# The TensorE program of a two-direction chunked scan, written as two counted loops, with the changes on VectorE and ScalarE that go with it

## The chip, the cores and the metric

The kernel runs on one core of one Trainium2 chip. The metric is the device time of one execution in microseconds (us). Three runs of the kernel before took 2723.7, 2718.01 and 2723.88 us; the median is 2723.7. The profiled execution took 2724.22 us by itself, and its trace spans 2722.2 us.

## The reference

The program is two transformer layers followed by one block of another kind, all in float32 on 256 tokens of width 1024. The change touches one piece of that last block, a recurrent scan over 16 heads of 64 channels, in two directions, first over 256 context tokens and then over 256 output tokens:

```python
def wkv_scan(s0, scan_in):
    def step(s, inp):
        w, kk, a, k, v, r = inp
        sa = jnp.einsum('dbhij,dbhj->dbhi', s, kk)
        s = s * w[..., None, :] - sa[..., :, None] * (kk * a)[..., None, :] + v[..., :, None] * k[..., None, :]
        return s, jnp.einsum('dbhij,dbhj->dbhi', s, r)
    return lax.scan(step, s0, scan_in)
...
    s_ctx, y_c = wkv_scan(s0, scan_c)
    _, y_x = wkv_scan(s_ctx, scan_x)
```

Only the outputs over the 256 output tokens (`y_x`) are used; of the context the scan hands on the state alone.

## The kernel before

The scan does 64 tokens at a time, so it has 8 steps `h`: 0 to 3 over the context (both directions `d` at once), 4 to 7 over the output tokens. The 16 heads lie as 8 chunks `c` of two heads, one head in partitions 0 to 63 and the other in 64 to 127, so a product for one direction is 16 small matmuls (`tile`, 64x64 by 64x64). Each float32 matmul appears in the trace as two weight loads (PEld) and two matmuls (PE), which makes four instructions on TensorE.

One step has these parts. `scores` multiplies keys, removal keys and a unit matrix; VectorE writes the part below the diagonal into `LA` (`left_matrices`, line 2644). GpSimd starts the inverse of a triangular matrix from it (`begin_inverse`, line 2985), VectorE transposes that start (line 2677), and then five levels follow, each a ring over four engines: TensorE multiplies `LA` by the present inverse (`left_products`), VectorE masks the product (line 2682, shown as L2400, the helper `tt`), TensorE multiplies again (`level_products`), ScalarE copies the result out of PSUM (line 2281), VectorE transposes it (line 2687). Four of the five levels are already a counted loop on TensorE (line 1923), whose waits compare a semaphore with a register; all its other waits before compare with a constant. When the inverse is done (`inverse_done`), `corrected_values` uses it, ScalarE copies the values out (line 2240), `state_update` sums the new state in PSUM, and VectorE adds it to the old state and scales it by the decay of the chunk (`new_state`, line 2665: two additions of 512 columns, one product of 1024). `uncorrected` of the next step needs that state. In steps 4 to 7 there are also `reads` (the masked matrices `RD`, line 2706) and the outputs (`first_outputs`, `last_outputs`). Two tiny copies on VectorE fetch the decay of the next step (`chunk_decay`, line 2572) between the fourth and the fifth level.

Every engine works its program in order. PSUM has 8 banks in two rings of four (`act_ring`, emptied by ScalarE, and `dve_ring`, emptied by VectorE); TensorE opens banks in turn and waits until a bank is free. On TensorE the eight steps stand one behind the other in the code; on the other engines too, before and after. The order of a step on TensorE:

```python
        for h in STEPS:
            read = h - 1 in X_STEPS
            if read:
                y = first_outputs(h - 1)
            if h:
                corrected_values(h - 1, h)
            if read:
                last_outputs(h - 1, y)
            if h:
                state_update(h - 1)
            ...
            scores(h, 0)
            scores(h, 1)
            ...
            inverse(h, left)
```

## Time and profile before

| | us |
|---|---|
| median of 3 runs (lowest, highest) | 2723.7 (2718.01, 2723.88) |
| the profiled execution, its own time | 2724.22 |
| its span in the trace | 2722.2 |
| TensorE busy | 2476.4 |
| VectorE busy | 1305.2 |
| ScalarE busy | 558.6 |
| GpSimd busy | 540.3 |

The page gives the busy time of each engine, the queues, the chain of work that ended last, and the costliest groups of instructions. The scan starts its first scores about 1517 us into the span and its last outputs are added at 1877 us. "Q8" below is the queue that the page calls q8 instruction: packets of the program itself that are fetched while it runs, 120 of them in this execution with 1.97 MB, so 16.4 KB each. A wait in a timeline is put in brackets with the idle time before it and what released it; "issue" stands for idle time for which the profile shows no releaser.

### The profile page before, as it was taken

The numbers are of one execution on the slowest core, as the hardware profiler recorded it, in microseconds if no ns is written. First come the engines' busy times: TensorE is split into PE (matmuls) and PEld (weight loads), VectorE is DVE, ScalarE is ACT, GpSimd is POOL, SyncE is SP. The second block draws the span as 40 slices with busy tenths as digits, with TensorE's granted clock in tenths as the row PEclk, the third lists the DMA queues.
The fourth block names the chain that finished last, engine by engine and source line by source line (L and its number), as shares of the span: only waits on it lengthen the run. The fifth ranks groups of instructions, "written<-read, shape, count | busy, mean of one in ns | idle before, by whom it ended". The sixth has DMA issues, their size and how long they took to land.

```text
span 2722.2 us, 43824 instructions
## 1 busy us (share of the span) xinstructions
PE 2476.4 (91%) x18216; PEld 1682.6 (62%) x18216; DVE 1305.2 (48%) x2899; ACT 558.6 (21%) x1285; POOL 540.3 (20%) x434
## 2 busy tenths in 40 slices
PE   8999999999999999998999787889998987787787
PEld 6688786476886853444677777878866533333333
DVE  2873310037732101147447554545228677777665
ACT  1243000013330000114333233222002111111111
POOL 0000000000000000000012665530003455544552
PEclk9999999999999999999999999999999999988999
DMA  5333333344233335423353011003348999999997
GB/s 189 148 120 124 131 151 152 133 168 157 102 124 143 149 148 218 162 93 135 144 201 78 18 32 34 18 3 133 124 170 319 414 415 421 421 421 422 422 421 319
DMA packets 91227, 523.70 MB, mean 192 GB/s; under 512 B 39728, under 2 KB 39728, under 8 KB 43440
## 3 DMA queue, kind: packets, MB, share of 16 engines
q0 software_dynamic: 39360, 277.51, 25.0%
q1 hardware_dynamic: 51696, 243.80, 24.0%
q8 instruction: 120, 1.97, 0.3%
q14 instruction: 51, 0.42, 0.0%
HBM read 511.85 MB, written 9.44 MB: 191 GB/s over the span
## 4 chain that ended last, share of the span: by engine, by line
PE 66%; DVE 13%; DMA 10%; issue 4%; ACT 2%; DVEq 2%; POOL 1%; POOLq 1%; ACTq 0%; SPq 0%
PE psum L523 35%; PE psum L1598 23%; DMA mem<-weights,mem 10%; DVE mem L2887 4%; PE psum L2045 3%; DVE mem L2400 2%; PE psum L765 2%; PE psum L539 1%; PE psum L2017 1%; POOL mem L2937 1%; DVE mem L2687 1%; ACT mem L2281 1%; POOL mem L3037 1%; DVEq L2521 0%; PE psum L1608 0%
## 5 line engine op out<-in xcount | busy, mean ns | idle before, releaser
L523 PE MATMUL psum<-mem 128*128 128x256 f32 (+10 forms) x4248 | 954.5, 397 | 7.5 <-DVE mem L1079 3.3
L1598 PE MATMUL psum<-mem 64*64 64x64 f32 (+6 forms) x12192 | 882.1, 273 | 85.6 <-DVEq L2683 23.2
L1598 PEld LDWEIGHTS psum<-mem 64*64 64x64 f32 (+3 forms) x12192 | 687.7, 154 | 279.1 <-issue 172.0
L523 PEld LDWEIGHTS psum<-mem 128*128 128x128 f32 (+5 forms) x4248 | 691.9, 182 | 262.5 <-issue 168.0
L2045 PE MATMUL psum<-mem 128*128 128x512 f32 x1024 | 496.4, 642 | 123.2 <-ACT mem L2364 123.1
L2045 PEld LDWEIGHTS psum<-mem 128*128 128x128 f32 x1024 | 205.0, 205 | 408.4 <-issue 241.0
L3037 POOL DMA_INDIRECT mem<-weights,mem x256 | 315.2, 1231 | 528.2 <-PE psum L2045 267.3
L2887 DVE CUSTOM_DVE_ANT_0 mem<-mem 128x1024 f32<-128x1024 f32 x256 | 307.3, 1224 | 138.8 <-DMA mem<-weights,mem 131.9
L2937 POOL TENSOR_TENSOR mem<-mem 128x512 f32<-128x512 f32 (+3 forms) x148 | 205.6, 1402 | 169.2 <-DVEq L2652 134.2
L2400 DVE TENSOR_TENSOR mem<-psum,mem 128x512 f32<-128x512 f32 (+1 forms) x145 | 97.3, 680 | 219.1 <-PE psum L1598 188.3
L2400 DVE TENSOR_TENSOR mem<-mem 128x512 f32<-128x512 f32 (+7 forms) x211 | 135.6, 651 | 89.0 <-ACTq L2153 67.5
L2359 ACT ACTIVATE mem<-mem 128x4 f32<-128x4 f32 (+2 forms) x70 | 14.4, 205 | 510.2 <-DVE mem L2891 510.2
L1284 DVE TENSOR_TENSOR mem<-mem 128x512 f32<-128x512 f32 x32 | 22.1, 692 | 193.7 <-ACTq L982 193.7
L1071 DVE SCALAR_TENSOR_TENSOR mem<-mem 128x256 f32<-128x256 f32 x240 | 105.6, 481 | 9.4 <-issue 0.9
L1304 POOL DMA_DIRECT2D mem<-vectors x1 | 0.5, 537 | 539.9 <-DVEq L1291 539.9
L1287 DVE TENSOR_TENSOR mem<-psum,mem 128x512 f32<-128x512 f32 x8 | 5.5, 692 | 205.5 <-PE psum L523 205.5
L1306 POOL MEMSET mem<- 128x256 f32 x1 | 0.3, 311 | 493.9 <-ACT mem L985 493.9
L3000 POOL DMA_DIRECT2D rates_dram<-mem x16 | 14.2, 892 | 405.9 <-DVEq L2570 405.9
L2364 ACT ACTIVATE mem<-mem 128x128 f32<-128x128 f32 x256 | 82.4, 390 | 32.7 <-DVE mem L2400 31.3
L2281 ACT ACTIVATE mem<-psum 128x512 f32<-128x512 f32 x80 | 47.8, 597 | 149.0 <-PE psum L1598 149.0
L2687 DVE STREAM_TRANSPOSE mem<-mem 128x512 f32<-128x512 f32 x64 | 45.5, 711 | 50.2 <-ACTq L2282 50.2
L837 ACT ACTIVATE mem<-psum 128x512 f32<-128x512 f32 (+4 forms) x88 | 45.7, 569 | 104.4 <-PE psum L523 100.2
(244 smaller groups left out, 1307.8 us busy)
## 6 DMA issues: line engine op xcount, KB each, us to landing
mem<-weights SPq DMA_DIRECT2D x100, 2048.0 KB, 7.4
rates_dram<-mem POOLq DMA_DIRECT2D x16, 512.0 KB, 5.0
mem<-rates_dram SPq DMA_DIRECT2D x32, 256.0 KB, 4.5
mem<-weights SPq DMA_DIRECT2D x7, 1024.0 KB, 6.7
mem<-weights SPq DMA_DIRECT2D x2, 2176.0 KB
mem<-weights,mem POOLq DMA_INDIRECT x256, 27.1
mem<-weights SPq DMA_DIRECT2D x2, 1536.0 KB, 8.5
mem<-weights SPq DMA_DIRECT2D x2, 1152.0 KB
```

Source lines behind the costliest of these rows:

```text
L523: ins = pe.matmul(out, lhsT, rhs, start=start, stop=stop, skip_group_check=skip)
L765: ins = pe.matmul(b, mg[:, k, t * P:(t + 1) * P], w[half][:, k, :], start=k == 0, stop=k == 7)
L1071: v.scalar_tensor_tensor(cacc[:, c, :], src, w, cacc[:, c, :], ALU.mult, ALU.add)
L1598: ins = pe.matmul(out, lhsT, rhs, start=start, stop=stop, skip_group_check=skip)
L2045: last = pe.matmul(psum[:, 4 + 2 * t + half, :], diag[:, n % DIAGS, :], rows_uv[buf_of[n]][:, D + half * 512:D + (half + 1) * 512], start= ...
L2281: A((Dm if j < LEVELS - 1 else DTm)[:, d * 512:(d + 1) * 512], banks[d], ACT.Copy)
L2364: A(diag[:, n % DIAGS, :], ident, ACT.Copy, scale=g1[:, n:n + 1]).then_inc(diag_ready.sem, 1)
L2400: return v.tensor_tensor(o, a, b, op)
L2687: v.transpose(DTm[:, d * 512:(d + 1) * 512], Dm[:, d * 512:(d + 1) * 512])
L2887: v.tensor_tensor_reduce(u, u, h2[:, t, :], 1.0, 0.0, ALU.mult, ALU.add, actp[:, n:n + 1])
L2937: return pool.tensor_tensor(o, a, b, op)
L3037: pool.indirect_dma_start(out=rows_uv[buf_of[n]], out_offset=None, in_=UV, in_offset=bass.IndirectOffsetOnAxis(ap=eidx_u[:, n:n + 1], axis ...
```

## The change

TensorE's program for the scan becomes two counted loops, one of four context steps and one of four output steps, with the loop over the levels inside. A step now begins with `scores` and ends with `state_update`, so the last step also updates the state and turns values that nobody uses; ScalarE and VectorE take those banks before they report the scan as done. Every wait in the loops compares with a register computed from the loop counters, and stands in an instruction of its own that also counts up a semaphore (`until`). So that each turn of a loop is alike: two more banks of `dve_ring` are opened and released in the output steps, the values of the next step are copied to a fixed place by ScalarE (`VS`, two copies of 512 columns, after the second level), and the old state enters the sum in PSUM through two 512-column products with the unit matrix (`kept_state`). VectorE then scales the sum straight out of PSUM (two operations of 512 columns in place of three). The decay of the next chunk is fetched by ScalarE behind its exponentials, no longer by VectorE in the inverse. VectorE's order within a level changes: transpose and mask of direction 0, then transpose and mask of direction 1. In the output steps the first transposes come before the masking of the second direction's reads.

```diff
...
+    VS = [zwa, sb2(512, base + 4096)]
...
+        step = {}
+
+        def at(signal, n, i=0):
+            return signal.sem, step["i"] * (step["steps"] * signal.per) + signal.at(step["h"] - n, i)[1]
+
+        def until(*waits):
+            for sem_, value in waits:
+                pe.wait_ge(sem_, value)
+            pe.sem_inc(pe_step, 1)
+
+        def bank(ring, tag):
+            tags = ring.filled["post"]
+            tags.append(tag)
+            n = len(tags) - 1
+            until((ring.free, step["i"] * step[ring] + ring.count("post", n)))
+            return ring.banks[:, n % 4, :]
+
         terms_done = [0]
 
         def mark(last):
             last.then_inc(term_full.sem, 1)
             terms_done[0] += 1
-            return terms_done[0]
+            return term_full.sem, step["i"] * step["terms"] + terms_done[0]
+
+        def staged_values(side, d, c):
+            return VS[d].rearrange("p (c n) -> p c n", c=8)[64 * side:64 * side + 64, c, :]
...
+        def kept_state():
+            b = [bank(dve_ring, "St") for _ in range(2)]
+            for d in range(2):
+                last = mm(b[d], ident, St[:, 512 * d:512 * d + 512], True, False, skip=True)
+            return b, mark(last)
+
+        def state_update(b, kept):
+            until(kept, at(u_ready, 0, 0))
             for c in range(8):
                 for head in range(2):
-                    tile(b[0], 0, c, head, 0, 0, own(TOK), half_of(nU), c == 0, False)
-                    last = tile(b[1], 1, c, head, 1, 0, other(TOK), half_of(VT_TOK), c == 0, False)
-            pe.wait_ge(term_full.sem, mark(last))
-            pe.wait_ge(*u_ready.at(h, 1))
+                    tile(b[0], 0, c, head, 0, 0, own(TOK), half_of(nU), False, False)
+                    last = tile(b[1], 1, c, head, 1, 0, other(TOK), half_of(VT_TOK), False, False)
+            until(mark(last), at(u_ready, 0, 1))
...
                 for d in range(2):
-                    pe.wait_ge(inverse_ready.sem, j * 2 + (2 * LEVELS * h + d + 1))
-                    pe.sem_inc(pe_step, 1)
+                    until(level(inverse_ready, 2, d))
                     left_products(left, d)
                 for d in range(2):
-                    pe.wait_ge(left_ready.sem, j * 2 + (2 * LEVELS * h + d + 1))
-                    pe.wait_ge(inverseT_ready[d].sem, j + (LEVELS * h + 1))
-                    pe.sem_inc(pe_step, 1)
+                    until(level(left_ready, 2, d), level(inverseT_ready[d], 1))
                     level_products(products[d], d, DTm, ARm)
...
-        for h in STEPS:
-            read = h - 1 in X_STEPS
+        def scan_step(read):
+            until(at(pq_ready, 0), at(k_ready, 0))
+            scores(0)
+            scores(1)
             if read:
-                y = first_outputs(h - 1)
-            if h:
-                corrected_values(h - 1, h)
+                reads(0)
+            uncorrected()
             if read:
-                last_outputs(h - 1, y)
-            if h:
-                state_update(h - 1)
-            if h == 0:
-                pe.wait_ge(*shift_parts_used.at(0, len(RW_ORDER) - 1))
-                values_product(h)
-            pe.wait_ge(*pq_ready.at(h))
-            pe.wait_ge(*k_ready.at(h))
-            scores(h, 0)
-            scores(h, 1)
-            if h in X_STEPS:
-                reads(h, 0)
-                uncorrected(h)
-                reads(h, 1)
-            else:
-                uncorrected(h)
-            left = [dve_ring.open(pe, "held") for _ in range(2)]
-            pe.wait_ge(*qt_ready.at(h, 1))
-            inverse(h, left)
-        y = first_outputs(7)
-        corrected_values(7)
-        last_outputs(7, y)
+                reads(1)
+            left = [bank(dve_ring, "held") for _ in range(2)]
+            until(at(qt_ready, 0, 1))
+            inverse(left)
+            if read:
+                for _ in range(2):
+                    bank(dve_ring, "held")
+                y = first_outputs()
+            kept = kept_state()
+            corrected_values()
+            if read:
+                last_outputs(y)
+            state_update(*kept)
+
+        pe.wait_ge(*shift_parts_used.at(0, len(RW_ORDER) - 1))
+        values_product(0)
+        for first, count, read, act_banks, dve_banks, terms in ((0, 4, False, 12, 8, 3), (4, 4, True, 12, 16, 5)):
+            filled = [len(ring.filled["post"]) for ring in (act_ring, dve_ring)]
+            with pe.Fori(0, count) as i:
+                step.update({"i": i, "h": first, "steps": 1, act_ring: act_banks, dve_ring: dve_banks, "terms": terms})
+                done = terms_done[0]
+                scan_step(read)
...
+            if h:
+                act.drain()
+                A(chunk_decays[h % 2][:, 0:8], R0[h % 2][:, 0, :, 63], ACT.Copy)
+                A(chunk_decays[h % 2][:, 8:16], R0[h % 2][:, 1, :, 0], ACT.Copy)
...
+                if j == 1 and h < 7:
+                    for d in range(2):
+                        A(VS[d].rearrange("p (c n) -> p c n", c=8), zv[:, :, starts(h + 1)[d]:starts(h + 1)[d] + 64], ACT.Copy)
...
+        for d in range(2):
+            take("Vt")
+            act.sem_inc(act_step, 1)
+        act.drain().then_inc(act_ring.free, 2)
...
-        def new_state():
+        def new_state(h):
             for d in range(2):
-                st = St[:, d * 512:(d + 1) * 512]
-                done(tt(st, take("St"), st, ALU.add))
-            v.drain()
-            tt(ch(St), ch(St), bc(Wc, 2, 64), ALU.mult)
+                kept = bc(chunk_decays[(h - 1) % 2][:, 8 * d:8 * d + 8], 2, 64)
+                done(tt(dir_(St, d), take("St").rearrange("p (c n) -> p c n", c=8), kept, ALU.mult))
             v.drain().then_inc(state_ready.sem, 1)
 
-        def inverse(h, between):
-            left = dve_ring.held(2)
+        def first_inverse(h):
             for d in range(2):
                 v.wait_ge(*inverseT_ready[d].at(h))
                 v.transpose(Dm[:, d * 512:(d + 1) * 512], DTm[:, d * 512:(d + 1) * 512])
                 v.drain().then_inc(inverse_ready.sem, 1)
+
+        def inverse(h):
+            left = dve_ring.held(2)
             for j in range(LEVELS):
                 for d in range(2):
+                    if j:
+                        v.wait_ge(*inverse_ready.at(h, 2 * j + d))
+                        v.transpose(DTm[:, d * 512:(d + 1) * 512], Dm[:, d * 512:(d + 1) * 512])
+                        v.drain().then_inc(inverseT_ready[d].sem, 1)
                     v.wait_ge(*left_full.at(h, 2 * j + d))
                     tt(dir_(ARm, d), left[d].rearrange("p (c n) -> p c n", c=8), bc(level[:, j + 1, 1 - d, :], 1, 8), ALU.mult)
                     v.drain().then_inc(left_ready.sem, 1)
-                if j < LEVELS - 1:
-                    for d in range(2):
-                        v.wait_ge(*inverse_ready.at(h, 2 * j + 2 + d))
-                        v.transpose(DTm[:, d * 512:(d + 1) * 512], Dm[:, d * 512:(d + 1) * 512])
-                        v.drain().then_inc(inverseT_ready[d].sem, 1)
-                between(j)
-            v.sem_inc(dve_ring.full, 2)
-            v.drain().then_inc(dve_ring.free, 2)
+            held = 2
+            if h in X_STEPS:
+                dve_ring.held(2)
+                held += 2
+            v.sem_inc(dve_ring.full, held)
+            v.drain().then_inc(dve_ring.free, held)
+
+        def read_matrices(h, d):
+            for head in range(2):
+                masked(f"reads{head}", RD[head], d, incl[:, d, :])
 
         for h in STEPS:
             if h - 1 in X_STEPS:
@@ -2696,22 +2737,21 @@
             if h in X_STEPS:
                 receptance(h)
             if h:
-                new_state()
-            v.tensor_copy(Wc, Wnext)
+                new_state(h)
             for d in range(2):
                 left_matrices(h, d)
             if h in X_STEPS:
-                for d in range(2):
-                    for head in range(2):
-                        masked(f"reads{head}", RD[head], d, incl[:, d, :])
+                read_matrices(h, 0)
+            first_inverse(h)
+            if h in X_STEPS:
+                read_matrices(h, 1)
                 v.drain().then_inc(intra_r_ready.sem, 1)
-
-            def next_rates(j):
-                if h < 7 and j == 3:
-                    chunk_decay(h + 1)
-
-            inverse(h, next_rates)
+            inverse(h)
         add_outputs(7)
+        for d in range(2):
+            take("St")
+            v.sem_inc(dve_step, 1)
+        v.drain().then_inc(dve_ring.free, 2)
```

The order on VectorE in an output step before, from the last state operation to the second level (L2400 that waits for dve_bank_full is `new_state` or the masking of `reads`, L2642 is `left_matrices`, L2677 the first transposes, L2687 the transposes of a level, L2400 that waits for left_full the mask of a level):

```order
L2400 TENSOR_TENSOR mem<-mem 128x1024
L2700 COPY mem<-mem 128x16
L2642 COPY_PREDICATED mem<-mem,psum 128x512 [waits dve_bank_full]
L2642 COPY_PREDICATED mem<-mem,psum 128x512 [waits act_bank_full]
L2642 COPY_PREDICATED mem<-mem,psum 128x512 [waits dve_bank_full]
L2642 COPY_PREDICATED mem<-mem,psum 128x512 [waits act_bank_full]
L2400 TENSOR_TENSOR mem<-psum,mem 128x512 [waits dve_bank_full] x4
L2677 STREAM_TRANSPOSE mem<-mem 128x512 [waits inverseT_ready0]
L2677 STREAM_TRANSPOSE mem<-mem 128x512 [waits inverseT_ready1]
L2400 TENSOR_TENSOR mem<-psum,mem 128x512 [waits left_full] x2
L2687 STREAM_TRANSPOSE mem<-mem 128x512 [waits inverse_ready] x2
L2400 TENSOR_TENSOR mem<-psum,mem 128x512 [waits left_full] x2
```

The same place after (L2435 is the helper that was L2400, L2709 the first transposes, L2718 those of a level):

```order
L2677 COPY_PREDICATED mem<-mem,psum 128x512 [waits act_bank_full]
L2435 TENSOR_TENSOR mem<-psum,mem 128x512 [waits dve_bank_full] x2
L2709 STREAM_TRANSPOSE mem<-mem 128x512 [waits inverseT_ready0]
L2709 STREAM_TRANSPOSE mem<-mem 128x512 [waits inverseT_ready1]
L2435 TENSOR_TENSOR mem<-psum,mem 128x512 [waits dve_bank_full] x2
L2435 TENSOR_TENSOR mem<-psum,mem 128x512 [waits left_full] x2
L2718 STREAM_TRANSPOSE mem<-mem 128x512 [waits inverse_ready]
L2435 TENSOR_TENSOR mem<-psum,mem 128x512 [waits left_full]
L2718 STREAM_TRANSPOSE mem<-mem 128x512 [waits inverse_ready]
L2435 TENSOR_TENSOR mem<-psum,mem 128x512 [waits left_full]
```

The masking of two of the four reads moved behind the first transposes, and in a level the masks and transposes now alternate.

On TensorE before, from the end of one context step's inverse to the next step's scores (first row: `corrected_values`; u_ready: `state_update`; 128x2x64: `scores`):

```order
L1598 MATMUL psum<-mem 64x64 [waits act_bank_free,inverse_done,u0_ready]
L1598 MATMUL psum<-mem 64x64 x29
L1598 MATMUL psum<-mem 64x64 [waits u0_ready,inverse_done]
L1598 MATMUL psum<-mem 64x64 x33
L1598 MATMUL psum<-mem 64x64 [waits u_ready,dve_bank_free]
L1598 MATMUL psum<-mem 64x64 x31
L1598 MATMUL psum<-mem 64x64 [waits u_ready,term_full]
L1598 MATMUL psum<-mem 64x64 x31
L1598 MATMUL psum<-mem 128x2x64 [waits dve_bank_free,act_bank_free,k_ready,pq_ready]
L1598 MATMUL psum<-mem 128x2x64 x15
```

The end of the same part after, where the loop (L1984) goes back; the scores stand at the head of the loop's body:

```order
L1599 MATMUL psum<-mem 64x64 [waits inverse_done,u0_ready]
L1599 MATMUL psum<-mem 64x64 x33
L1805 REGISTER_ALU
L1599 MATMUL psum<-mem 64x64 [waits term_full,u_ready]
L1599 MATMUL psum<-mem 64x64 x31
L1805 REGISTER_ALU
L1599 MATMUL psum<-mem 64x64 [waits term_full,u_ready]
L1599 MATMUL psum<-mem 64x64 x31
L1984 REGISTER_ALU
L1984 COMPARE_AND_BRANCH
```

And the head of that body after, up to the first scores, which the branch leads back to:

```order
L1984 ISA
L1805 ISA [waits pq_ready,k_ready]
L1805 REGISTER_ALU [waits dve_bank_free]
L1805 ISA [waits dve_bank_free]
L1805 REGISTER_ALU [waits act_bank_free]
L1599 MATMUL psum<-mem 128x2x64 [waits act_bank_free]
L1599 MATMUL psum<-mem 128x2x64 x15
```

Ahead of the scores there are now a branch and a row of register operations and waits. Counted out, the body of the context loop is 354 matmuls and 75 other instructions, 1491 in all with four to a matmul; that of the output loop 482 matmuls and 101 others, 2029 in all. The body of the inner loop is 64 matmuls, some 265 instructions.

## Rows read from the trace of the kernel before

**Rows 1.** The page: TensorE in all, and the queue that fetches the program.

```profile
PE 2476.4 (91%) x18216; PEld 1682.6 (62%) x18216; DVE 1305.2 (48%) x2899; ACT 558.6 (21%) x1285; POOL 540.3 (20%) x434
...
q8 instruction: 120, 1.97, 0.3%
```

**Rows 2.** Busy time by stretch: us, engines busy (instructions), granted clock, DMA share, GB/s.

```profile
1510.00:1880.00 370.00, 299.24 (x9616) 285.57 (x9617) 186.55 (x274) 111.63 (x177) 183.15 (x131) 0.95 0.11 27
...
1743.00:1751.00 8.00, 5.65 (x128) 5.47 (x127) 4.09 (x6) 2.93 (x4) 6.80 (x7) 0.79 0.35 70
1751.00:1769.00 18.00, 15.60 (x500) 15.13 (x497) 11.47 (x18) 4.21 (x8) 13.32 (x8) 1.00 0.01 1
```

**Rows 3.** Timeline of one level (start, us, engine, instructions, idle before).

```profile
1575.40 4.03 PE L1598 MATMUL psum<-mem 64*64 64x64 f32 x128 [0.53 <-DVEq L2683]
...
1577.24 0.71 DVE L2687 STREAM_TRANSPOSE mem<-mem 128x512 f32<-128x512 f32 x1 [1.30 <-ACTq L2282]
1577.52 0.60 ACT L2281 ACTIVATE mem<-psum 128x512 f32<-128x512 f32 x1 [0.34 <-PE psum L1598]
1578.17 0.71 DVE L2687 STREAM_TRANSPOSE mem<-mem 128x512 f32<-128x512 f32 x1 [0.22 <-ACTq L2282]
1579.00 1.50 DVE L2400 TENSOR_TENSOR mem<-psum,mem 128x512 f32<-128x512 f32 x2
...
1580.00 4.03 PE L1598 MATMUL psum<-mem 64*64 64x64 f32 x128 [0.57 <-DVEq L2683]
```

**Rows 4.** The chain that ended last, over the fifth level and a context step's end.

```profile
1589.01 0.69 DVE mem L2400
...
1589.79 2.11 PE psum L1598 x64
...
1593.05 1.17 PE psum L1598 x60
...
1594.92 8.47 issue
1603.39 1.30 POOLq L2994
```

**Rows 5.** Timeline of the same boundary: TensorE's gap, the state and the scores.

```profile
1598.07 4.46 PE L1598 MATMUL psum<-mem 64*64 64x64 f32 x95 [1.08 <-issue]
1598.81 1.29 DVE L2400 TENSOR_TENSOR mem<-psum,mem 128x512 f32<-128x512 f32 x2 [8.29 <-PE psum L1598]
...
1600.19 1.23 DVE L2400 TENSOR_TENSOR mem<-mem 128x1024 f32<-128x1024 f32 x1
1601.54 0.17 DVE L2700 COPY mem<-mem 128x16 f32<-128x16 f32 x1
1601.65 0.73 DVE L2642 COPY_PREDICATED mem<-mem,psum 128x512 f32<-128x512 uint32 x1
```

**Rows 6.** The groups of VectorE's two small copies, 1510 to 1880 us.

```profile
L2574 DVE COPY mem<-mem 128x8 f32<-128x8 f32 x7 | 5.2, 748 | 1.2 <-issue 0.5
...
L2575 DVE COPY mem<-mem 128x8 f32<-128x8 f32 x7 | 1.1, 161 | 0.0
```

**Rows 7.** Timeline of an output step, from GpSimd's start of the inverse to the first mask.

```profile
1740.30 2.59 POOL L2937 TENSOR_TENSOR mem<-mem 64x512 f32<-64x512 f32 x2 [0.24 <-issue]
...
1743.59 1.29 DVE L2400 TENSOR_TENSOR mem<-psum,mem 128x512 f32<-128x512 f32 x2 [2.96 <-PE psum L1598]
...
1745.91 7.56 PE L1598 MATMUL psum<-mem 64*64 64x64 f32 x192 [2.35 <-DVEq L2678]
1747.91 0.69 DVE L2400 TENSOR_TENSOR mem<-psum,mem 128x512 f32<-128x512 f32 x1 [1.35 <-PE psum L1598]
```

**Rows 8.** The chain over an output step's end, from the outputs to the scores.

```profile
1774.70 1.75 issue
1776.45 3.02 PE psum L1598 x124
1779.46 1.01 issue
...
1782.44 0.67 DVE mem L2400
...
1785.26 0.74 DVE mem L2642
```

**Rows 9.** The instruction queue from 1591 to 1606 us.

```profile
q8 instruction: 4, 0.07, 2.0%
```

**Rows 10.** All queues from 1854 to 1867 us, three turns of the inner loop.

```profile
DMA packets 0, 0.00 MB, mean 0 GB/s; under 512 B 0, under 2 KB 0, under 8 KB 0
```

**Rows 11.** The group of products of 512 columns.

```profile
L2045 PE MATMUL psum<-mem 128*128 128x512 f32 x1024 | 496.4, 642 | 123.2 <-ACT mem L2364 123.1
```

**Rows 12.** Timeline at the end of the scan: last outputs added, and yT's first use.

```profile
1876.63 0.69 DVE L2400 TENSOR_TENSOR mem<-psum,mem 128x512 f32<-128x512 f32 x1 [0.24 <-PE psum L1598]
...
1906.27 1.00 DVE L2741 TENSOR_SCALAR mem<-psum,mem 128x256 f32<-128x256 f32 x2 [11.26 <-PE psum L1598]
```

95 lines of the change are left out of this document (46 added, 49 removed).

## The prediction

> **What bounds the kernel now.** I read the page first. TensorE is busy for 2476.4 of 2722.2 us [rows 1], so what counts is TensorE's own time and what it waits for. The change touches only the scan, so I then read the busy time by stretch. Between 1510 and 1880 us no engine is full: TensorE 299 of 370 us, VectorE 187, GpSimd 183, ScalarE 112 [rows 2]. Such a stretch is set by latencies around a ring of engines, and the gain or loss of an edit has to be read where it stands in that ring.
>
> The timeline of one level shows the ring [rows 3]: TensorE's products of 128 records (two level products, two left products) take 4.03 us, 1.01 for one direction; ScalarE copies the second result at 1577.52, VectorE transposes it at 1578.17, masks from 1579.00, and TensorE goes on at 1580.00, 4.60 us after the last such start at 1575.40. TensorE idles 0.57 us of it.
>
> The chain over a context step's end shows 8.47 us for which the profile names no releaser [rows 4]. The timeline fills them in [rows 5]: TensorE has a gap of 1.08 us in the middle of work that waits for nobody, then comes the state (two operations in 1.29 us, one of 1.23, a copy), and only at 1601.65 does VectorE take the scores. The gap has a cause in another view. From 1591 to 1606 us the queue that fetches the program moves four packets, one in 3.75 us [rows 9]. Over the whole kernel 120 packets [rows 1] serve 36,432 loads and matmuls, less three repeats of eight inner loops (24 x 256 = 6144) and plus some 500 others: 30,800 instructions, 256 to a packet. TensorE uses nearly as many in 3.02 us (124 matmuls and as many loads [rows 8]), faster than they come, so straight code of small matmuls runs dry at packet borders. In the output steps the chain has two such pauses, 1.75 and 1.01 us [rows 8]. And in three turns of the inner loop (1854 to 1867 us) not one packet is fetched [rows 10]: a body of 265 instructions, which always lies over two packets, stays where it is although the packet behind it has been fetched too. So at least three packets are kept.
>
> **The change part by part.** I sum against the profiled execution, 2724.22 us; the median of the three runs is 0.5 lower, which changes nothing.
>
> The decay copies leave VectorE: in 1510 to 1880 us seven pairs, 5.2 + 1.1 = 6.3 us busy [rows 6], and 0.15 us of drains and waits with each. They stand between the fourth and the fifth level, on the ring. That is 6.3 + 7 x 0.15 = 7.4 us gained. On ScalarE the two copies come behind the exponentials of the next step, where it waits for the first level anyway. Bounds: 0 (if something else is late) to 7.4. I take 7.4, since each copy is followed at once by the mask that TensorE waits for.
>
> The reads of direction 1 go behind the first transposes. Today GpSimd has the second start ready at 1740.30 + 2.59 = 1742.9, but VectorE masks two reads at 1743.59 first, TensorE idles 2.35 us, starts its left products at 1745.91, and these run slowly, because the granted clock in this stretch is 0.79 and in the next 1.00 [rows 2, 7]; so the mask comes only at 1747.91. After the change the transposes are done by 1743.7, TensorE starts at about 1744.3 behind its waits, the mask can follow at 1745.5: 2.4 us. The other three output steps start the same way with less lost to the clock (1.4 to 2.0). Sum 7.3 us gained, bounds 4 and 10.
>
> The level's new order on VectorE: mask 0, transpose 1, mask 1 are now in a row behind the first left product. That product ends at 1575.40 + 3 x 1.01 = 1578.43, mask 0 starts at 1578.55, the next two each 0.83 later (as 1578.17 to 1579.00), mask 1 ends at 1580.9, and the second level product runs from 1581.0 to 1582.0; today it ends at 1580.00 + 2.02 = 1582.0 [rows 3]. The early start of the first product is given away by the second. I count 0.1 us lost for a level, 4 x 8 x 0.1 = 3.2 us, bounds -5 and +8.
>
> The waits. In the inner loop, which compares with registers today, TensorE starts 0.31 us after a mask ends (1579.00 + 0.69 to 1580.00), in the fifth level, with constants, 0.10 (1589.01 + 0.69 to 1589.79) [rows 3, 4]. So a released wait costs 0.2 us more, two or three times in a step in the fifth level and behind it: 0.5 us, 4.0 us in eight steps. A row of waits that are already met costs about 0.1 us an instruction where TensorE has nothing queued; ahead of the scores there are ten, 0.7 us after what is hidden.
>
> The boundary of a context step. The two products with the unit matrix are four passes of 496.4 / 1024 = 0.485 us [rows 11], 1.94 us. The wait for ScalarE before `corrected_values` (1591.90 to 1593.05 [rows 4]) hides 1.1, so that starts 0.85 us later. Without packet gaps (the body being kept) the sum of the state ends at about 1598.2 and not at 1598.6 (5.55 us from there today, 1.3 of it gaps: 1593.9 + 4.25); VectorE needs 1.3 us for the state in place of 2.8 and is ready at 1599.7; but the scores begin at 1598.95 behind the branch and the waits, and their first half takes 2 us. VectorE takes them at 1600.9 in place of 1601.65 [rows 5]: 0.75 us gained, three times, and 0.3 at the first boundary: 2.5 us. The VectorE saving of 1.5 us is cut to half because TensorE becomes the late one.
>
> The boundary of an output step, three times. Here all hangs on whether the loop's body is still there when the branch goes back 2029 instructions, 7.9 packets. If it is not, the branch waits for a packet (3.75 us by [rows 9]), and as the body begins near the end of one, soon for a second. The pauses of 1.75 and 1.01 us [rows 8] take in the 1.94 us of unit products, so the state's sum ends about 1.3 us earlier, at 1780.9. Then come 7.5 us of fetching, less 0.9 for what TensorE has queued, and 2.9 us of scores: 1790.4, where it is 1786.1 today. VectorE was 1.1 us later than the scores [rows 8], so 3.2 us are lost each time, 9.6 us. If it is there: the sum ends at 1779.5, the scores at 1784.1, and 2.3 us are gained each time.
>
> The end. The last step now also forms the unit products (1.94), turned values (32 matmuls more, 1.05) and the state (64 matmuls, 2.1): 5.1 us, of which 0.4 in waits. From 1876.63 on [rows 12] TensorE goes into long products at once, and yT waits for these and not for VectorE; nothing hides it. 4.7 us lost. ScalarE's two staging copies fall in 3 us in which it waits for TensorE: nothing.
>
> Sum: -7.4 - 7.3 + 3.2 + 4.0 - 2.5 + 9.6 + 4.7 = +4.3 us. 2724.2 + 4.3 = 2728.5 us, about 2728.
>
> The gaps and the silent inner loop show that a packet costs 3.75 us and that two lie behind [rows 9, 10]. The Trainium skill, page "Runtime: NRT & Kernel Launch", section "Instruction fetch mechanics", says both that only two blocks are held and that TensorE has room for 2048 instructions in blocks of 256. By two blocks the inner loop would have to fetch; the trace disagrees. By 2048 the context body stays, and the output body, which lies over nine blocks, does not: an estimate by that rule is the sum above.
>
> **The rivals.** (A) Both bodies are kept. For it: the inner loop shows keeping without any limit. Against it: the output body is eight times what the trace shows kept. Term -7.0 in place of +9.6: -12.3, 2712 us. (B), slower: neither is kept. For it: the trace shows nothing beyond three packets. Place: the branch back of the context loop, three times; price: one packet of 3.75, as the body begins at the start of one, less 0.75 queued, so +3 us each. Decides if fewer than seven packets are held. +4.3 + 9 = 2738 us. (C) The register waits cost more than their 0.2 us because they stand in rows (75 instructions of this kind in a context body, 101 in an output body): if 20 more of them are bare in each step at 0.1 us, 16 us, 2744 us. Against it: most stand where TensorE waits for another engine anyway.
>
> **How the numbers follow.** Between 265 instructions kept and 2029 not known, the rows leave the limit open; the context body (1491) and the output body split it, and a limit between the two or above both is as likely as the rows can say, below both less, since holding three packets and no more would be a close fit to the one case seen. A measurement of this kernel tells a change of 0.3%, 8 us, from none. Forecast 0.38 (of that 0.03 faster, 0.24 same, 0.11 slower), A 0.30 (0.24 faster, 0.06 same), B 0.20 (0.18 slower, 0.02 same), C 0.12 (0.02 same, 0.10 slower). Together faster 0.27, same 0.34, slower 0.39. The forecast's own range is 2720 to 2736; for eight in ten it must reach A and most of B and C: 2706 to 2745.
>
> **What would show it.** In the trace after, fetched packets by stretch: about seven for the first context step, none for the next three (B: some); about eight for each output step and a pause of TensorE of 4 to 7 us ahead of the scores of steps 5, 6 and 7 (A: none, and no pause). VectorE's first mask in an output step 3 us after GpSimd's second start, not 5. No mask held up behind two small copies. Scores end later than the state operations. A level of 4.6 to 4.8 us. The last outputs to the first long product 5 us longer. I would be wrong in the sum if a level were longer than 5 us or shorter than 4.4, since that counts 32 times.

## The result, and the profile after

The changed kernel takes 2747.3 us (median of 4 runs, 2741.8 to 2749.5), the kernel before 2723.8; the ratio is 1.0092 with a 95% interval of 1.0074 to 1.0110. It is slower by 23.5 us in the medians, and by 17.6 us in the profiled executions (span 2739.8 against 2722.2). 2728 had been forecast, 2706 to 2745 as the range.

First the page, TensorE in all and the queue that fetches the program, to be read beside [rows 1]:

```profile
PE 2501.1 (91%) x18440; PEld 1694.1 (62%) x18440; DVE 1289.2 (47%) x2870; ACT 568.9 (21%) x1313; POOL 537.2 (20%) x434
...
q8 instruction: 112, 1.84, 0.3%
```

Three context bodies of some 1491 instructions and three output bodies of some 2029 went out of the code, about 41 packets of 256, and only 8 fetches with them. One of the loops must still be fetching its body in every turn. To find which, I divide the scan at one landmark that both kernels have: the start of VectorE's last transpose of a step (`v.transpose` of the second direction ahead of the fifth level). The distances are the lengths of the steps, in us; the first column starts at VectorE's first transpose of the scan. The packets are the starts on the instruction queue from one step's first transpose to the next step's, for step 8 up to the last outputs added (1876.63 and 1890.42 us).

| | step 1 | 2 | 3 | 4 | 5 | 6 | 7 | 8 | last transpose to yT's use | packets by step |
|---|---|---|---|---|---|---|---|---|---|---|
| before | 22.9 | 41.0 | 40.2 | 41.6 | 47.7 | 49.2 | 49.7 | 50.9 | 39.6 | 6, 6, 5, 7, 8, 7, 8, 4 |
| after | 23.3 | 41.0 | 39.8 | 39.8 | 42.5 | 54.6 | 55.0 | 59.3 | 44.8 | 5, 0, 0, 2, 10, 9, 10, 6 |

Steps 1 to 5 gain 7.0 us, steps 6 to 8 lose 19.1, the end loses 5.2. The packets say why: the context body is fetched once and kept, the output body is fetched anew each time. That is the case forecast. What it costs is not.

The chain over one output step's end answers to [rows 8]:

```profile
1779.71 0.67 DVE mem L2435
1780.38 0.61 DVEq L2704
1780.99 4.25 issue
1785.24 9.48 PE psum L1599 x158
```

No engine releases TensorE in these 4.25 us. In the record of instructions its branch at the loop's end stands from 1779.31 to 1783.94 us, and then five waits that are already met take until 1785.2. The same stretch by the granted clock (us, busy time and instructions of PE, PEld, DVE, ACT, POOL, clock, DMA share, GB/s):

```profile
1779.70:1784.00 4.30, 0.00 (x0) 0.00 (x0) 1.28 (x2) 1.08 (x2) 0.00 (x0) 0.94 0.03 4
1784.00:1785.20 1.20, 0.00 (x0) 0.00 (x0) 0.00 (x0) 0.00 (x0) 0.00 (x0) 0.50 0.06 14
1785.20:1790.50 5.30, 5.26 (x46) 5.05 (x48) 0.85 (x2) 0.27 (x1) 0.00 (x0) 0.52 0.02 3
1790.50:1794.70 4.20, 4.18 (x120) 3.98 (x116) 3.22 (x5) 2.12 (x4) 3.18 (x3) 1.00 0.01 2
```

This is what the prediction left out. TensorE had been granted its full 2.4 GHz; behind the pause it has 1.2 GHz (0.50) until shortly before 1790.5, and the scores, which are next, are slow: 46 matmuls in 5.3 us. In a kernel without the pause (short_aligned, below) 64 of the same take 3.84 us.

In the last step something else is added. A 2 MB weight transfer starts in its first half, and later TensorE stands idle for 3.36 us for nothing that the profile shows:

```profile
1847.17 0.34 SPq L1575 DMA_DIRECT2D mem<-weights  x1
...
1856.17 8.57 PE L1599 MATMUL psum<-mem 64*64 64x64 f32 x192 [3.36 <-issue]
```

Its queue starts no packet between 1843.9 and 1852.2 us, and TensorE goes on 4.0 us after that last start: it seems to have lacked this packet. The DMA share (the last number but one) and the clock ahead of it show the transfer and, behind the pause, 0.50 again:

```profile
1848.00:1849.00 1.00, 1.00 (x59) 0.93 (x61) 0.88 (x3) 0.60 (x1) 0.76 (x2) 1.00 1.19 262
...
1853.00:1854.00 1.00, 0.00 (x0) 0.00 (x0) 1.00 (x2) 0.00 (x0) 0.00 (x0) 1.00 0.65 262
...
1856.00:1858.00 2.00, 1.83 (x34) 1.86 (x36) 0.00 (x0) 0.00 (x0) 0.00 (x0) 0.50 0.03 8
```

The other terms of the sum have their lines too. A level, to be read with [rows 3]: the second mask comes behind the second transpose, and the next start is 4.76 us after the last (1580.17 - 1575.41), where it was 4.60:

```profile
1575.41 4.41 PE L1599 MATMUL psum<-mem 64*64 64x64 f32 x128 [0.34 <-DVEq L2722]
...
1577.66 0.69 DVE L2435 TENSOR_TENSOR mem<-psum,mem 128x512 f32<-128x512 f32 x1 [1.19 <-PE psum L1599]
1578.47 0.71 DVE L2718 STREAM_TRANSPOSE mem<-mem 128x512 f32<-128x512 f32 x1
...
1579.30 0.69 DVE L2435 TENSOR_TENSOR mem<-psum,mem 128x512 f32<-128x512 f32 x1
...
1580.17 0.27 PE L1599 MATMUL psum<-mem 64*64 64x64 f32 x2 [0.35 <-DVEq L2722]
```

The context boundary, with [rows 5]. The state is two operations that also scale it, nothing follows them, and VectorE takes the scores at 1600.23; TensorE begins them 1.11 us after its last product, behind the branch and five met waits:

```profile
1597.02 1.29 DVE L2435 TENSOR_TENSOR mem<-psum,mem 128x512 f32<-128x512 f32 x2 [7.65 <-PE psum L1599]
...
1598.10 3.84 PE L1599 MATMUL psum<-mem 64*128 64x128 f32 x64 [1.11 <-DVE mem L2435]
1600.23 0.73 DVE L2677 COPY_PREDICATED mem<-mem,psum 128x512 f32<-128x512 uint32 x1 [1.92 <-PE psum L1599]
```

The turned reads, with [rows 7]. GpSimd's second start ends at 1794.05 + 2.59 = 1796.64, the first mask comes 3.6 us later; before it was 5.0:

```profile
1794.05 2.59 POOL L2977 TENSOR_TENSOR mem<-mem 64x512 f32<-64x512 f32 x2 [0.24 <-issue]
...
1799.08 5.13 PE L1599 MATMUL psum<-mem 64*64 64x64 f32 x151 [0.90 <-issue]
...
1800.27 0.69 DVE L2435 TENSOR_TENSOR mem<-psum,mem 128x512 f32<-128x512 f32 x1 [0.79 <-PE psum L1599]
```

And the end, with [rows 12]: the last outputs are added at 1890.42, yT is first used at 1923.62, 44.83 us after the last transpose (1878.79), where it was 39.6:

```profile
1890.42 0.69 DVE L2435 TENSOR_TENSOR mem<-psum,mem 128x512 f32<-128x512 f32 x1 [10.11 <-PE psum L1599]
...
1923.62 0.99 DVE L2781 TENSOR_SCALAR mem<-psum,mem 128x256 f32<-128x256 f32 x2 [11.69 <-PE psum L1599]
```

### The profile page after: what moved, and what is told of

Read it like the earlier page. It is cut to its first block, busy times and chain, and to the rows that moved or that the text cites. A ratio compares the mean times of both kernels' runs of the same rounds, so it can differ in the third digit from the quotient of the medians.

```text
span 2739.8 us, 44728 instructions
## 1 busy us (share of the span) xinstructions
PE 2501.1 (91%) x18440; PEld 1694.1 (62%) x18440; DVE 1289.2 (47%) x2870; ACT 568.9 (21%) x1313; POOL 537.2 (20%) x434
## 4 chain that ended last, share of the span: by engine, by line
PE 68%; DVE 12%; DMA 10%; issue 4%; DVEq 1%; POOL 1%; ACT 1%; POOLq 1%; ACTq 0%; SPq 0%
PE psum L523 34%; PE psum L1599 24%; DMA mem<-weights,mem 9%; PE psum L2069 5%; DVE mem L2927 4%; DVE mem L2435 3%; PE psum L765 2%; PE psum L539 1%; PE psum L2041 1%; POOL mem L2977 1%; DVE mem L2718 1%; POOL mem L3077 1%; PE psum L1609 1%; DVEq L2556 0%; DMA mem<-weights 0%
## 5 line engine op out<-in xcount | busy, mean ns | idle before, releaser
L1599 PE MATMUL psum<-mem 64*64 64x64 f32 (+8 forms) x12416 | 900.8, 270 | 83.4 <-issue 26.2
L1599 PEld LDWEIGHTS psum<-mem 64*64 64x64 f32 (+4 forms) x12416 | 695.1, 151 | 288.2 <-issue 208.2
L2435 DVE TENSOR_TENSOR mem<-psum,mem 128x512 f32<-128x512 f32 (+1 forms) x145 | 97.3, 680 | 239.2 <-PE psum L1599 212.2
L2435 DVE TENSOR_TENSOR mem<-mem 128x512 f32<-128x512 f32 (+7 forms) x204 | 127.1, 631 | 89.0 <-ACTq L2177 67.5
L2394 ACT ACTIVATE mem<-mem 128x4 f32<-128x4 f32 (+2 forms) x70 | 14.3, 205 | 511.3 <-DVE mem L2931 511.3
L2309 ACT ACTIVATE mem<-psum 128x512 f32<-128x512 f32 x80 | 47.8, 597 | 127.2 <-PE psum L1599 127.2
L837 ACT ACTIVATE mem<-psum 128x512 f32<-128x512 f32 (+4 forms) x88 | 45.6, 569 | 104.4 <-PE psum L523 100.2
L981 ACT ACTIVATE mem<-psum 128x512 f32<-128x512 f32 x32 | 19.1, 597 | 201.5 <-PE psum L523 201.5
```

Of the source, the lines that this page charges most:

```text
L837: return A(dst, src(b) if src else b, func).then_inc(act_ring.free, 1)
L1599: ins = pe.matmul(out, lhsT, rhs, start=start, stop=stop, skip_group_check=skip)
L2309: A((Dm if j < LEVELS - 1 else DTm)[:, d * 512:(d + 1) * 512], banks[d], ACT.Copy)
L2435: return v.tensor_tensor(o, a, b, op)
```

## The experiments

Ahead of the scan all kernels are alike but for semaphore increments in three of them, and yet VectorE's first transpose of the scan lies between 1519 and 1532 us in the profiled runs. The increments cost time of their own: TensorE idles 7.8 to 9.4 us ahead of the first product of the scan in these three, and 3.7 in the changed kernel, so their whole times hold some 4 to 6 us that have nothing to do with the loop. A cause is therefore read from the lengths of the steps, and whether a kernel is faster from the repeated runs, as a ratio to the kernel before. The step lengths are those of one profiled execution of each kernel, so a difference of a microsecond or two in a single step proves little. "Sum" is the eight steps of the table above: 343.2 us before, 355.3 after.

**Which loop costs it.** In the code that calls `scan_step` the loop is replaced by the steps written out, for the output steps, for both, or for the context steps:

```
+            if read:        # both: if True; context alone: if not read
+                for h in range(first, first + count):
+                    step.update({"i": 0, "h": h, ...})
+                    scan_step(read)
+                continue
             with pe.Fori(0, count) as i:
```

> The context steps stay one counted loop, the four output steps are written out on TensorE; all else as in the changed kernel. Theory (the way back of the output loop: three pauses of 4.3 us until the program is there again, and behind each the scores at the lower clock, about 2.2 us, in the last step a weight transfer in the way of a program packet as well): the output steps take 47 to 49 us and not 55, and the run is 15 to 25 us faster than the changed kernel, 2716 to 2726 us. No TensorE clock of 0.5 ahead of the scores of steps 5 to 7. Rival (the register waits and the level's order cost it, the loop itself is cheap): within 5 us of the changed kernel, 2738 to 2747.

Measured: 2720.8 us (11 runs), ratio 0.9995 (0.9986 to 1.0004). Steps 6 to 8 take 49.5, 47.7 and 52.8 us; the sum is 335.1, 20.2 less than with the loop, and the granted clock of steps 6 and 7 as a whole is 1.00. The theory holds for the run and for steps 6 and 7, within 0.5 us of the 47 to 49 expected; the last step stays longer, at 52.8.

> Both loops are written out on TensorE, with constants in the waits outside the inner loop; all else as in the changed kernel. Theory: against the run with only the output steps written out it loses what the kept context body gains in packet gaps, 1 us in each of three steps, and gains a little on the waits: 0 to 5 us slower than that run. Rival (register waits in rows cost more than the gaps): 3 us or more faster than that run.

Measured: 2723.5 us, ratio 1.0003 (0.9993 to 1.0013), sum 336.6. The theory's 0 to 5 us more are met, with 1.5 us of steps and 2.7 us in the medians; but the two intervals overlap, so this gain of the context loop is not clear of noise.

> The context steps are written out, the output steps stay a counted loop. Theory: the three pauses of the output loop stay, so the time is that of the changed kernel or up to 5 us more, 2742 to 2750 us. Rival (the register waits of any loop cost it): about half of the loss of the changed kernel goes, 2730 to 2736 us.

Measured: 2749.1 us, ratio 1.0106 (1.0090 to 1.0122), steps 6 to 8 54.7, 54.1 and 57.4. So the loss of the counted loops, against the same steps written out, is the output loop's.

**How much program is kept.** The fifth level goes into the inner loop, which makes both bodies shorter by 263 instructions. This kernel leaves the inverse untransposed, so its outputs are not those of the scan; the instructions, tiles and waits of a step stay the same in kind, and only its times are used. Semaphore increments ahead of the scan move the body against the packets' borders (the diff is shortened):

```
-            with pe.Fori(0, LEVELS - 1) as j:      # and the fifth level's code behind it
+            with pe.Fori(0, LEVELS) as j:
...
+        for _ in range(58):                        # short_aligned; out_aligned: 48, all else as changed
+            pe.sem_inc(pe_step, 1)
         pe.wait_ge(*shift_parts_used.at(0, len(RW_ORDER) - 1))
```

> The changed kernel with the fifth level taken into the inner loop (its last product has its operands the other way round, so the inverse is left untransposed), which makes the output body 1766 instructions, and 58 semaphore increments far ahead of the scan, so that this body lies over seven program packets. Theory (eight packets are held, one of them fetched ahead): the body is kept, no packets in steps 6 to 8, no pause at the way back, output steps of 47 to 49 us in place of 55, the run 17 to 23 us faster than the changed kernel, 2718 to 2726. Rival (no more than the six packets of the context body and the one behind are held): packets and pauses as in the changed kernel, 2740 to 2748.

Measured: 2725.0 us, ratio 1.0011 (1.0001 to 1.0021). An estimated 5.7 us of it are the bare increments (TensorE idles 9.35 us ahead of the scan, where the changed kernel has 3.66). Steps 6 to 8 take 47.6, 47.6 and 47.4 us with no packet in them, and the page has 80 packets:

```profile
q8 instruction: 80, 1.31, 0.2%
```

> The same body of 1766 instructions without the increments, so that it lies over eight program packets. Theory (eight held, one of them ahead): the ninth pushes the first out, and so every packet is fetched anew: some nine packets in each output step, pauses of 4 us, 2738 to 2746 us. Rival (size counts, not the packets that it touches: 2048 instructions are held): no packets in steps 6 to 8 and 2718 to 2726 us.

Measured: 2743.3 us, ratio 1.0072 (1.0054 to 1.0089), steps of 54.8, 54.7 and 58.3 us. The same code, begun 58 instructions earlier, is fetched again. Over step 7 (1765 to 1820 us) its queue shows:

```profile
q8 instruction: 9, 0.15, 1.3%
```

> The changed kernel with 48 semaphore increments far ahead of the scan, so that the output body of 2029 instructions lies over eight packets and not nine. Theory (eight held, one of them ahead): as the changed kernel, 2740 to 2748 us. Rival (eight held beside the one ahead): kept, no packets in steps 6 to 8, 2720 to 2728 us.

Measured: 2746.3 us, ratio 1.0090 (1.0068 to 1.0111), steps of 54.0, 53.7 and 58.2 us, 9 packets in step 7. A body of 2029 instructions over eight packets is not kept. So a body over seven is kept, one over eight is not, whatever its length in instructions. The number fetched in a turn is the body's packets and one more (9 for eight; 10, 9 and 10 for the nine of the changed kernel), so the reading that fits is room for eight packets, of which the packet behind the loop's end, fetched ahead, takes one; the runs show the border between seven and eight, and this split only by inference. The Trainium skill's figure (page "Runtime: NRT & Kernel Launch", section "Instruction fetch mechanics") of room for 2048 instructions in blocks of 256 agrees with these runs if one block is taken up in this way; its other figure in the same section, two blocks, does not.

**What the pause does.** Idle time without fetching, ahead of the scores of steps 6, 7 and 8, in the kernel with the output steps written out:

```
+                    if h > first:
+                        for _ in range(60):        # idle28: 28
+                            pe.sem_inc(pe_step, 1)
```

> As the run with the output steps written out, but ahead of the scores of steps 5, 6 and 7 TensorE goes through 60 bare semaphore increments, an idle time of 3 to 6 us in which no program is fetched beyond the usual. Theory (the clock falls behind an idle TensorE and the scores then run at half speed): each place costs its idle time and 1.5 to 2.5 us more, together 14 to 24 us over that run, and the clock behind it is 0.5 to 0.8. Rival (the slow scores come from program packets being fetched one by one behind the branch): only the idle time is lost, the clock stays 1.0 and the scores take as long as without it.

Measured: 2753.3 us, ratio 1.0124 (1.0107 to 1.0141), steps of 59.6, 59.9 and 62.1 us, 10.1, 12.2 and 9.3 more than without. That is 32.5 us over out_straight, above the 14 to 24 expected. The idle time is longer than expected, 9.5 us, since one bare increment takes 0.155 us, and it explains nearly all: beyond it the three places cost 0.6, 2.7 and nothing, where 1.5 to 2.5 each had been expected. The clock is 0.50 from 1726 us on, and the scores begin with it, so the clock fell as expected and its price does not show in this kernel's steps.

> As the run with 60 bare increments ahead of the scores of steps 5 to 7, but 28, which at 0.155 us each make 4.3 us, the length of the changed kernel's pause. Theory: the clock falls to 0.5 behind this idle time too, and the steps are 6 to 7 us longer than in the run without increments (4.3 idle, 2.2 for the slow scores). Rival (it takes the 9.5 us of idle time of that run to lower the clock): 4.0 to 4.5 us longer, the clock stays 1.0.

Measured (one execution, 2731.7 us): steps of 55.4, 52.0 and 55.2 us, 5.9, 4.3 and 2.4 more than without, not 6 to 7. The clock does fall:

```profile
1722.00:1724.00 2.00, 0.00 (x0) 0.00 (x0) 0.00 (x0) 0.00 (x0) 0.00 (x0) 1.00 0.00 0
1724.00:1726.00 2.00, 0.76 (x6) 0.79 (x8) 0.00 (x0) 0.00 (x0) 0.00 (x0) 0.64 0.00 0
1726.00:1728.00 2.00, 2.00 (x24) 2.00 (x22) 0.00 (x0) 0.00 (x0) 0.00 (x0) 0.50 0.00 0
```

In written-out code waits for packets mix with it, so the size could not be read here. It can in a body that is kept, the one over seven packets (again with the inverse left untransposed):

```
+            if read:
+                with pe.Fori(0, 10):
+                    pe.sem_inc(pe_step, 1)
             until(at(pq_ready, 0), at(k_ready, 0))
             scores(0)
```

> The run with the body of 1766 instructions over seven packets (the inverse again untransposed), with ten turns of a loop of one semaphore increment ahead of the scores of each output step, some 4 us of idle TensorE, in a body that is kept. Theory (the way back costs its pause and, through the clock, 2.2 us of slow scores, whoever causes the idle time): no packets in steps 6 to 8, a clock of 0.5 at the scores, and each output step longer than the 47.5 us of the kept body by the idle time and 2.0 to 2.5 us, some 54 us, as in the changed kernel. Rival (slow scores belong to fetching): longer by the idle time alone, 51.5 us, clock 1.0.

Measured: 2751.8 us, ratio 1.0108 (1.0088 to 1.0128), steps 6 to 8 of 55.4, 54.8 and 54.7 us and no packets in them. TensorE's rows around the scores of step 6, first with the ten turns and then in the kept body without them:

```profile
1746.32 9.41 PE L1599 MATMUL psum<-mem 64*128 64x128 f32 x160 [6.56 <-issue]
```

```profile
1736.35 3.84 PE L1599 MATMUL psum<-mem 64*128 64x128 f32 x64 [1.21 <-ACT mem L2264]
```

5.35 us of idle time are added. The scores and the first reads then take 9.4 us; in the kept body they run from 1736.4 to 1743.7, 7.3. The step is longer by 7.2 to 7.9 us, about 5.35 + 2.1. The clock with the ten turns:

```profile
1742.00:1746.00 4.00, 0.00 (x0) 0.00 (x0) 0.00 (x0) 0.00 (x0) 0.00 (x0) 0.50 0.00 0
1746.00:1752.00 6.00, 5.68 (x53) 5.71 (x55) 1.46 (x2) 0.60 (x2) 0.04 (x1) 0.50 0.00 0
1752.00:1756.00 4.00, 3.82 (x116) 3.65 (x117) 2.67 (x4) 1.79 (x3) 3.70 (x3) 0.99 0.03 7
```

So the slow scores belong to the idle time, not to fetching.

**The transfer in the last step.** On SyncE, ahead of the weight transfer, a wait for the transpose of direction 0 in the first level (the first of the levels' transposes, and not the second as the expectations call it):

```
                 sp.wait_ge(*lt_ready.at(7, 1))
+                sp.wait_ge(*inverseT_ready[0].at(7, 1))
```

> The changed kernel with the 2 MB weight transfer of the last output step held back until VectorE's second transpose of that step's levels. Theory (of the 59.3 us of the last step 4 come from this transfer, which delays a program packet, and from the lower clock behind that pause): the last step 54 to 56 us, the run 3 to 5 us faster, 2738 to 2744 us. Rival (the last step is longer for another reason): 58 to 60 us and no change.

Measured: 2745.5 us, ratio 1.0084 (1.0057 to 1.0111), last step 56.8 us in place of 59.3, but steps 6 and 7 took 57.1 and 55.9 in this run. The last step is now like its neighbours, as the theory has it, but 56.8 us is above the 54 to 56 expected, 2745.5 above the 2738 to 2744, and a gain of the whole is not shown.

**The level's order.** VectorE's loop as before, on top of the written-out output steps:

```
             for j in range(LEVELS):
-                for d in range(2):
-                    if j: ... transpose d
-                    ... mask d
+                if j: for d in range(2): ... transpose d
+                for d in range(2): ... mask d
```

> As the run with the output steps written out, with VectorE's order in a level as in the kernel before (both masks, then both transposes). Theory (the new order costs 0.12 us a level because the second level product waits for three operations in a row): a level of 4.57 to 4.60 us in place of 4.71, 32 levels, 3 to 5 us faster than that run. Rival (the 0.12 us are the waits against registers, since the order gives and takes the same): the level stays at 4.7 us or gets longer, the time is the same within 2 us or worse.

Measured: 2717.7 us, ratio 0.9982 (0.9972 to 0.9993), 3.1 us less, by intervals that overlap; the sum is 331.5 in place of 335.1. The mean distance of VectorE's transposes from level to level is 4.59 us in place of 4.69 (4.71 in the changed kernel, 4.58 before). In this run the context steps are a counted loop, which compares every wait with a register computed from both loop counters; the output steps are written out. From the transpose of direction 0 ahead of the third level to that ahead of the fourth, a context step takes 4.62 us here and 4.57 in straight_trimmed_late, where it is written out with the same order. With the new order it takes 4.75 us counted (the changed kernel) and 4.66 written out (both_straight). So the waits of a counted step cost 0.05 to 0.09 us in a level, and the order 0.09 to 0.13.

**The last step.** On top of that, nothing is computed that nobody reads:

```
+            more = step["h"] < 7
+            if more: kept = kept_state()
+            corrected_values(more)                 # turned values only if more
...
+            if more: state_update(*kept)
```

> The run with the output steps written out and the old order of a level, and in the last step neither the products with the unit matrix, nor the turned values, nor the state. Theory (these products stand bare at the end): the stretch behind the last step's levels, 861.7 us there, is 4 to 6 us shorter, 2711 to 2715 us, faster than the kernel before by 0.3 to 0.4%. Rival (ScalarE and VectorE are the late ones there, or the first long product waits for its weights): under 2 us.

Measured: 2711.4 us, ratio 0.9952 (0.9936 to 0.9968). The stretch behind the levels is 857.9 us, 3.8 less, a little under the 4 to 6 expected; to yT's use it is 41.8 us and not 45.3. In the last step a pause for a packet shows again, beside the weight transfer:

```profile
1825.22 2.19 PE L1599 MATMUL psum<-mem 64*128 64x64 f32 x19 [3.04 <-issue]
```

> As the run before, and the 2 MB weight transfer that now starts at the last step's left matrices is held back until VectorE's second transpose of that step's levels. Theory (that transfer delays program packets in the last output step, which takes 51 to 53 us and not 47.5 to 49): the last step 2 to 4 us shorter, the stretch behind it no longer, 2708 to 2713 us. Rival (the last step is long for its own reason, or the weights now come late): within 1 us of that run or slower.

Measured: 2708.7 us, ratio 0.9940 (0.9924 to 0.9956), last step 47.1 us in place of 52.6; steps 6 and 7 are 48.0 and 48.8 where they were 47.1 and 47.4, and the two intervals overlap, so the gain is shown for the last step and not for the whole. The pause is gone:

```profile
1820.33 8.46 PE L1600 MATMUL psum<-mem 64*128 64x64 f32 x256 [0.20 <-issue]
```

**The two reorderings alone,** in the kernel before: ScalarE copies the decays into one of two buffers and VectorE's copies go; or `first_inverse` is called between the masks of the reads of direction 0 and 1.

```
+            if h:                                  # ScalarE, behind decays(h); copies_only
+                A(chunk_decays[h % 2][:, 0:8], R0[h % 2][:, 0, :, 63], ACT.Copy)
+                A(chunk_decays[h % 2][:, 8:16], R0[h % 2][:, 1, :, 0], ACT.Copy)
...
                 masked(reads, d=0)                 # VectorE; reads_only
+            first_inverse(h)
                 masked(reads, d=1)
```

> The kernel before, with only the decay copies moved to ScalarE and the copy of the kept decays left out. Theory: each of seven steps is 1.0 us shorter between the fourth and the fifth level, 6 to 8 us in all, 2715 to 2718 us. Rival (something else is late at that place): 0 to 2 us.

Measured: 2714.7 us, ratio 0.9960 (0.9946 to 0.9974), sum 333.1, 10.1 less, more than the 6 to 8 expected.

> The kernel before, with only the masks of direction 1's reads behind the first transposes. Theory: 1.4 to 2.4 us less in each of the four output steps, 6 to 9 us, 2714 to 2719 us. Rival (TensorE reaches its left products at the same time because it or GpSimd is late): under 2 us.

Measured: 2712.9 us, ratio 0.9964 (0.9952 to 0.9977), sum 331.6, 11.6 less, 10.9 of it in the four output steps (4.7, 0.9, 2.9, 2.4), more than the 6 to 9 expected. The clock may have a part in this. In the kernel before, the left products that begin 2.35 us late [rows 7] run at half clock, and step 5, where the edit gives most, has a granted clock of 0.89 as a whole; with the edit it has 1.00. First two stretches of the kernel before, then the same step in reads_only:

```profile
1747.00:1749.00 2.00, 2.00 (x43) 2.00 (x42) 0.69 (x1) 0.00 (x0) 1.85 (x3) 0.50 0.01 3
...
1669.10:1716.80 47.70, 38.52 (x1157) 37.05 (x1154) 25.51 (x36) 13.95 (x22) 27.92 (x20) 0.89 0.11 24
```

```profile
1671.10:1714.10 43.00, 35.30 (x1159) 33.65 (x1156) 25.45 (x36) 13.97 (x22) 25.81 (x19) 1.00 0.12 27
```

How much of the gain is the clock's was not measured apart.

> The kernel before with both single edits, the decay copies on ScalarE and the reads of direction 1 behind the first transposes. Theory (the two gains add up: 10.1 us of steps for the one, 11.6 for the other): the eight steps are 18 to 22 us shorter than before, 2701 to 2706 us. Rival (both shorten the same waits or lose to program packets that come late): 12 us or less, 2710 us or more.

Measured: 2703.2 us, ratio 0.9919 (0.9905 to 0.9933), sum 325.1, 18.1 less. The gains add up but for 3.6 us; output steps 6 to 8 take 46.3, 44.8 and 46.8 us, with a clock of 1.00, where it was 0.97, 0.97 and 0.93.

> The same with the 2 MB weight transfer of the last step held back until the first level's transposed inverse. Theory: 0 to 3 us less in the last step, since in this kernel the packets of that step fall mostly clear of it. Rival: the later weights are waited for behind the scan, 1 to 3 us slower.

Measured: 2701.4 us, ratio 0.9915 (0.9898 to 0.9932), last step 45.9 in place of 46.8. The lowest time of the study, not told apart from the run before it.

> The run with late weights and no extra products in the last step, with the context steps written out as well: no counted loop but the inner one. Against the run with both single edits it still has the kept state through products with the unit matrix, the staged values and a semaphore increment with each wait. Theory (kept state and increments cost what the loop form needs, about 1 us a step of 8): 4 to 10 us slower than the kernel with both single edits and late weights, 2706 to 2712 us. Rival (the kept state saves VectorE as much as it costs TensorE): the same within 2 us.

Measured: 2711.7 us, ratio 0.9954 (0.9940 to 0.9967), output steps 6 to 8 of 47.0, 47.1 and 48.0 us against 45.8, 44.4 and 45.9. Against copies_reads_late, the form that a loop needs (the kept state summed on TensorE, staged values, an increment with each wait) costs 10.3 us by the medians even where no step loops, at the upper end of the 4 to 10 expected: 4.6 us are in the steps and 4.8 in the stretch behind them (860.4 us against 855.6). Which of its parts does was not tried.

## Why the prediction was wrong

The sign of the largest term was right and its mechanism too: the context body kept, the output body not, a pause ahead of the scores of steps 6 to 8. The size was not. The step that failed is the term of the output boundary, +9.6, built on "Then come 7.5 us of fetching, less 0.9 for what TensorE has queued, and 2.9 us of scores": it left the clock out, put the kept boundary 2.3 us under today's, and had no term for the last step's weight transfer.

- **The output boundary, +9.6.** All terms together gave steps 6 to 8 +3.4 us (-3.2 copies, -5.7 reads, +1.2 levels, +1.5 waits, +9.6); they measured +19.1. The miss of 15.7 has three parts, which together make some 15. First, a kept step: the sum implied 45.6 us for it (49.9 on average before, less 1.06, 1.9 and 2.3, plus 0.4 and 0.5), short_aligned measured 47.5, three times 1.9. The copies and reads are not to blame: in copies_reads these three steps are 46.0 on average, 4.0 less than before, where 3.0 was forecast. The loop's form is: from there to the kept body it adds 1.6 us a step, where the prediction had -1.4 (-2.3 for the kept boundary, +0.4, +0.5), and which part of the form does it stays open. Second, what a body that isn't kept adds: 5.5 us forecast, 7.3 and 7.1 measured (from 47.6 and 47.6 in short_aligned to 54.8 and 54.7 in short_unaligned, the same code). In this the fetching was put too high (one pause of 4.6 us at the branch and 1.2 of waits behind it, 5.8, not the 6.6 of two packets in a row), and the clock was left out: 2.1 us of slow scores each time (kept_idle, 9.4 us in place of 7.3), though [rows 2, 7] showed a clock of 0.79 behind 2.35 us of idle time, and I had used that for the reads. Third, the last step: 59.3 us, 4.5 more than its neighbours, beside the weight transfer (52.6 to 47.1 us with the transfer held back, trimmed to trimmed_late).
- **The copies, -7.4.** Alone they give 10.1 us of steps, more than the bound. Of this 2.1 and 2.9 are in steps 4 and 5, where the copies themselves are 0.9 each. In step 5 the granted clock as a whole goes from 0.89 to 0.92 with it, which may be a part; in step 4 it is 1.00 in both, and why that step gains more was not traced.
- **The reads, -7.3.** Alone 10.9 us in the four output steps, a little over the bound of 10. The two together give 18.1. The prediction used a clock of 0.79 for the one place that it had a row for; the kernel before lies under 1.00 in seven of its eight steps (0.89 in step 5), and what an edit gives back through the clock had no term.
- **The level's order, +3.2.** 0.09 to 0.13 us in a level, 3.6 us of steps (out_straight to old_order). Right.
- **The register waits, +4.0.** They were put at nothing in the first four levels, and cost 0.05 to 0.09 us in one (old_order); the 0.2 us for a released wait in the fifth was not measured apart. In rows one met wait takes 0.25 us (five from 1784.1 to 1785.2), a bare increment with constants 0.155: 1.1 us ahead of each step's scores, where 0.7 was counted.
- **The context steps, -2.5 at the boundaries.** VectorE takes the scores 12.4 us after the last transpose and not 14.3: 1.9 less, 1.06 of it the copies, so 0.85 where 0.75 was forecast. Steps 1 to 5 gained 7.0 in place of 3.8; in the changed kernel their clock is 1.00 throughout, before it was 0.93, 0.96, 0.96, 1.00 and 0.89, which the sum did not count.
- **The end, +4.7.** 5.2 to yT's use; leaving the products out gives back 3.6. Right.

Of the rivals, A did not occur in the changed kernel, and where its body is kept (short_aligned) the time is 2725.0 and not A's 2712. Of these 13 us, 5.7 are the bare increments ahead of the scan and 5.7 the steps 6 to 8 of the first part above, so a kept body alone would be near 2719 us (an estimate), not told apart from the kernel before. B did not occur: no packet from 1557 to 1678 us. C named the right size of the total for a wrong reason. The range ended 2 us under the median; the mechanisms were varied in it and never the clock.

## What to carry to other kernels

Before a loop is put around code, count its instructions in packets of 256 from where it really starts: here a body over seven packets fetched nothing and one over eight paid in every turn the pause of the branch and the slow work at half clock behind it. A new pause of TensorE of some us is to be priced together with the slow work behind it, and a pause that an edit takes away is worth more than its length for the same reason. And a change made of several edits should be taken apart: here two edits of a few lines are worth 20 us, and the loops and what they need take that and 23 more.

## What the runs showed of the hardware that I had not expected

- A body over seven packets of 256 instructions fetched nothing in three turns (short_aligned), one over eight 9 packets a turn, with 1766 instructions (short_unaligned) as with 2029 (out_aligned). That fits room for eight packets, one of which goes to the packet behind the loop.
- A branch to a packet that is not there held TensorE for 4.3 to 4.6 us in the changed kernel (1724.5 to 1728.7, 1779.3 to 1783.9, 1834.5 to 1838.8), for 3.4 to 3.6 in out_aligned and for 4.6 to 4.7 in short_unaligned; one to a packet that is there held it for 0.2 (short_aligned).
- After 4.6 us of idle time that no fetch caused (28 increments), the granted clock was 0.50 while TensorE was fully busy from 1726 to 1730 us, as after the branch. In the kernel before it was 0.50 from 1747 to 1749 us, behind 2.35 us of idle time.
- While a weight transfer kept the DMA engines 0.65 to 1.19 busy, TensorE stood for 3.36 us, and for 3.04 us beside the same transfer in trimmed; with the transfer held back the pause was 0.20 us.
